# Asking for the second-layer expert weights on ScalarE's queue in a hybrid decoder block

## The reference, cut to what matters

```python
def clamped_swiglu(u):
    glu, lin = jnp.split(u, 2, axis=-1)
    glu = jnp.minimum(glu, SWIGLU_LIMIT)
    lin = jnp.clip(lin, -SWIGLU_LIMIT, SWIGLU_LIMIT)
    return glu * jax.nn.sigmoid(SWIGLU_ALPHA * glu) * (lin + 1.0)

def expert_block(args):
    xblk, e = args
    u = xblk @ w1[e] + b1[e]                 # w1[e]: 1024 x 2048, 8.39 MB
    return clamped_swiglu(u) @ w2[e] + b2[e] # w2[e]: 1024 x 1024, 4.19 MB
...
return jnp.einsum('tkd,tk->td', yb[slot].reshape(t, TOP_K, d), gates)
```

## Time and profile before

| | us |
|---|---|
| median of 3 runs | 1315.1 (1312.94 to 1317.31) |
| the profiled execution, its own time | 1317.5 |
| its span | 1315.7 |
| experts' part, start of the first expert's first layer to the end of the span | 387.4 to 1315.7 |
| DMA rate in the experts' part | 429 to 430 GB/s |

### The profile page before, as it was taken

One profiled execution on the slowest core, in us unless ns is written; L12 is line 12 of the kernel. 1 busy time (PEld: TensorE's weight loads), 2 busy tenths in 40 slices (PEclk: granted clock), 3 DMA queues, 4 the chain that ended last, 5 costly groups with the idle time before them and its releaser, 6 DMA issues.

```text
span 1315.7 us, 23661 instructions
## 1 busy us (share of the span) xinstructions
PE 1226.7 (93%) x10440; PEld 637.8 (48%) x10441; DVE 308.0 (23%) x615; ACT 214.9 (16%) x346; POOL 55.9 (4%) x33
## 2 busy tenths in 40 slices
PE   8999999999999999998989989898988989898897
PEld 6777888888653433333433333343333333343332
DVE  2464433233151211111111111121111111121112
ACT  4531221311040110010100000010100001110001
POOL 0800120000020000000000000000000000000000
PEclk9999999999989999999999999999999999999999
DMA  9521232246779999999999999999999999999994
GB/s 301 192 69 61 89 109 67 67 130 225 319 291 391 422 434 424 430 429 430 435 426 434 422 432 427 430 430 431 428 429 432 428 431 429 432 430 428 433 426 205
DMA packets 55077, 450.03 MB, mean 342 GB/s; under 512 B 5808, under 2 KB 23728, under 8 KB 35472
## 3 DMA queue, kind: packets, MB, share of 16 engines
q1 hardware_dynamic: 51936, 446.85, 82.0%
q10 hardware_dynamic: 3088, 2.37, 0.7%
HBM read 448.16 MB, written 1.05 MB: 341 GB/s over the span
## 4 chain that ended last, share of the span: by engine, by line
PE 64%; DMA 31%; DVE 3%; issue 1%; ACT 0%; SPq 0%; DVEq 0%
DMA ring<-in_exp_w 31%; PE ps L1061 21%; PE sums L557 17%; PE ps L1096 10%; PE sums L1036 3%; PE ps L1026 2%; PE sums L643 2%; PE ps L643 2%; PE sums L941 1%; PE ps L941 1%; PE ps L645 1%; PE ps L1074 1%; DVE work L2034 1%; PE ps L1083 1%; PE ps L1003 1%
## 5 line engine op out<-in xcount | busy, mean ns | idle before, releaser
L1061 PE MATMUL ps<-ring,work 128*64 128x512 f32 x2048 | 468.5, 615 | 49.3 <-DMA ring<-in_exp_w 48.5
L1061 PEld LDWEIGHTS ps<-ring,work 128*64 128x64 f32 x2048 | 155.0, 141 | 346.8 <-issue 295.9
L557 PE MATMUL sums<-work,ring 128*128 128x256 f32 (+1 forms) x1120 | 243.3, 384 | 0.6 <-DVE work L1564 0.6
L1096 PE MATMUL ps<-ring,work 128*64 128x512 f32 x1024 | 225.1, 592 | 0.0
L557 PEld LDWEIGHTS sums<-work,ring 128*128 128x128 f32 (+1 forms) x1120 | 199.7, 186 | 33.1 <-issue 3.5
L1422 ACT ACTIVATE work<-work 128x512 f32<-128x512 f32 x32 | 20.1, 629 | 733.7 <-DVE work L2023 733.7
L2023 DVE TENSOR_SCALAR work<-ps 128x512 f32<-128x512 f32 x32 | 22.1, 692 | 496.7 <-PE ps L1061 496.7
L1096 PEld LDWEIGHTS ps<-ring,work 128*64 128x64 f32 x1024 | 72.5, 136 | 129.6 <-issue 129.6
L2039 DVE COPY work<-ps 128x512 f32<-128x512 f32 x32 | 22.1, 692 | 208.2 <-PE ps L1096 208.2
L1026 PEld LDWEIGHTS ps<-sel,work 128*128 128x128 bf16 x1536 | 53.7, 118 | 24.3 <-issue 24.3
L1036 PE MATMUL sums<-work 64*128 64x512 f32 x256 | 63.6, 615 | 0.0
(11 more groups left out here) (275 smaller groups left out, 792.6 us busy)
## 6 DMA issues: line engine op xcount, KB each, us to landing
ring<-in_exp_w SPq DMA_DIRECT2D x112, 2048.0 KB, 30.4
ring<-in_exp_w SPq DMA_DIRECT2D x40, 4096.0 KB, 29.3
ring<-in_w_in SPq DMA_DIRECT2D x8, 2048.0 KB, 9.5
ring<-in_w_in SPq DMA_DIRECT2D x16, 1024.0 KB, 7.4
ring<-in_w_out SPq DMA_DIRECT2D x2, 2048.0 KB, 9.9
ring<-in_w_in SPq DMA_DIRECT2D x1, 1152.0 KB, 7.7
work<-in_x SPq DMA_DIRECT2D x2, 512.0 KB, 4.6
work<-in_x ACTq DMA_DIRECT2D x2, 512.0 KB, 4.0
```

The lines of the kernel that those rows point to most:

```text
L557: last = mm(bank_of(b)[width * g:width * g + width, 0:T], chunk(n)[:, k, c0:c0 + width], XN[:, k, :], start=k == 0, stop=k == KT - 1)
L1061: last = mm(ps[4 + part][64 * half:64 * half + 64, :], xe[:, k * CAP:(k + 1) * CAP], ring[:, slot(u, k), part * D + half * 512:part * D + ...
L1096: last = mm(ps[7][64 * half:64 * half + 64, :], lhs, ring[:, slot(u, 8 + j), i * D + half * 512:i * D + half * 512 + 512], start=False, st ...
```

## The change

The function `load_w2` moves out of SyncE's stream and takes the engine that asks as its first argument. SyncE keeps every first-layer block, and the second-layer block of expert 0. The second-layer blocks of the experts 1 to 31 are asked for by ScalarE: in the turn of expert e, right behind the sigmoid and ahead of the copies of `xe` and `actT`, two halves of C of expert e+1, with the same waits on `w_used` as before (22 and 24 counted from the expert's turn, which is 10 and 12 of the expert after). Since places and semaphores depend on the expert's number modulo 4, ScalarE's loop over the 32 experts is written out in fours, and the last four stand behind the loop, where the last expert asks for nothing.

```diff
+        def load_w2(eng, e, u, j):
+
+            g = group(u, 2)
+            src = exp_w2[0, bass.ds(e, 1), j * 4 * P:(j + 1) * 4 * P, :].rearrange(
+                "a (p s) n -> p (a s n)", s=4)
+            dst = ring[:, GROUP[g] + 2 * j:GROUP[g] + 2 * j + 2, :].rearrange("p s n -> p (s n)")
+            eng.dma_start(dst, src).then_inc((group_in, w2_half_in)[j][g], 16)
...
-            def load_expert(e, it, u, first_j=0):
+            def load_expert(e, it, u, first_j=0, second=False):
...
-                for j in range(2):
-
-                    sp.wait_ge(w_used, it * 12 + 2 * j + 10)
-                    load_w2(e, u, j)
+                if u == 0 and second:
+                    for j in range(2):
+
+                        sp.wait_ge(w_used, it * 12 + 2 * j + 10)
+                        load_w2(sp, e, u, j)
...
-                    with sp.Fori(0, E // 4) as i:
+                    for u in range(4):
+                        load_expert(u, r * E + u, u, 0, u == 0)
+                    with sp.Fori(1, E // 4) as i:
...
-                with act.Fori(0, E) as e:
-                    it = r * E + e
+                def take_expert(it, e, u, following=True):
+
                     act.wait_ge(glu_ready, it + 1)
                     af(sig, glu, ACT.Sigmoid, scale=ALPHA).then_inc(sig_ready, 1)
+                    if following:
+                        for j in range(2):
+                            act.wait_ge(w_used, it * 12 + 2 * j + 22)
+                            load_w2(act, e + 1, (u + 1) % 4, j)
                     act.wait_ge(gathered, it + 2)
                     af(xe, ps[6][:, :], ACT.Copy).then_inc(xe_ready, 1)
                     act.wait_ge(act_turned, it + 1)
                     af(actT, ps[4][:, :], ACT.Copy).then_inc(at_ready, 1)
+
+                with act.Fori(0, E // 4 - 1) as i:
+                    for u in range(4):
+                        take_expert(r * E + i * 4 + u, i * 4 + u, u)
+                for u in range(4):
+                    take_expert(r * E + (E - 4 + u), E - 4 + u, u, u < 3)
```

More of the change, by code:

```diff
@@ L479, in _ @@
             load_w1(0, 0, 1)
-            load_w2(0, 0, 1)
+            load_w2(sp, 0, 0, 1)
             sp.wait_ge(blk_done, len(blocks))
@@ L483, in _ @@
             sp.wait_ge(w_used, 16)
-            load_w2(0, 0, 0)
+            load_w2(sp, 0, 0, 0)
             load_w1(1, 1, 0, 1)
```

## The result

The changed kernel took 1327.15 us (median of 6 runs, 1322.85 to 1330.21) where the kernel before took 1316.12 (6 runs on the same chips): a ratio of 1.0078 with a 95% interval of 1.0065 to 1.0092, so 8.6 to 12.1 us slower. The forecast was 9 us slower, 1324 from a median of 1315.1. The profiled execution took 1328.85 us, its span is 1327.0, 11.3 us over that of before. Six executions of the changed kernel spread over 7 us, so of a single trace a us or two can be chance.

A forecast was written before the change was run, and what follows sets the result against it. The experts' part was taken as bound by DMA bytes at 430 GB/s. Terms 0 (ScalarE), 0 (later asks), 0 (SyncE) and +9.0 (byte order) on the median of 1315.1 gave 1324 us, range 1309 to 1333.

The forecast's parts named there:

- ScalarE's time: Two asks per expert, 0.75 us, fit in ScalarE's 2.3 us of idle time between sigmoid and copy: 0 us.
- Rival 4: ScalarE is held by its asks, so copies and second layer come late: up to 22 us, 1337 us; chance 0.03.
- Asks later: Second-layer asks go out 4.8 and 1.8 us later for expert 31, but the DMA engines do not run dry: 0 us.
- SyncE's side: SyncE loses two asks and two waits per expert, but no first-layer block is asked for sooner: 0 us.
- The order of the bytes: On its own queue, second-layer block C overtakes first-layer block B, so PE's first layer of expert 31 ends later: +9.0 us.
- Rival 1: Both DMA queues are served as one common line in order of asking, so nothing moves: 1315 us; chance 0.13.
- hand sum: Block arrivals worked: C of expert 31 through first, last half of B seen by PE at 1298.6: +9.0 us.
- D: The end of the weight transfers, put at 1296.2 us and expected to stay there.
- the way from D to the last landing: Time from the end of transfers until PE sees the last block: 2.4 us, 1296.2 to 1298.6.
- the two steps behind that landing: Two first-layer steps of expert 31 left on PE after B's last half: 3.5 us, ending at 1302.1.
- rival 3: DMA rate falls 1% from queue switching, 1333 us, or PE's lowered clock costs up to 3 us, 1327; chance 0.09.
- Rival 2: Two queues raise the DMA rate; 1% is worth 8.8 us: 1306 with order kept, 1315 with order turned; chance 0.15.

The follow-up runs named there:

- the pair of experiments: Changed kernel with only experts 1 to 28's second-layer blocks on ScalarE's queue: 1317.22 us, ratio 1.0002 to the kernel before; with only 29 to 31's: 1326.57 us, 1.0076.
- the experiment with three experts: Changed kernel with second-layer blocks of experts 1 to 28 on SyncE's queue, only 29 to 31 on ScalarE's: 1326.57 us, ratio 1.0076 to the kernel before.

## Why the prediction was right

*ScalarE's time, 0.* Right: sigmoid to copy unchanged at 2.90 us. The two asks take 0.82 us together (0.75 forecast). Rival 4 is out.

*Asks later, 0.* Right, and shown by itself: asks 5.4 and 2.6 us later on one queue give 1.0003.

*SyncE's side, 0.* Nothing in the traces speaks of a gain there. It was not tested alone.

*The order of the bytes, +9.0.* Right in mechanism and place. C at a half or a third of the rate: 116 packets to 116, 73 to 66. The waits begin at 505 us (near 500 forecast), sit on B, and the last one ends at 1299.1 (1298.6 forecast), two steps ahead of the end of the first layer. The loss is a lead that is lost once: moved back for the last three experts it is gone, made for the last three alone it is whole. Rival 1, one common line, is out by the packet counts and by the pair of experiments. One step of the hand sum came out otherwise, at no cost: C was not through first, but landed beside B (1299.3 and 1299.1).

*The size.* By the medians it is 11.0 us for 9.0. By the traces two terms were too small. The traces are to be compared from the start of the experts' part, since the part ahead of it, which the change does not touch, was 1.35 us shorter in the changed kernel's trace (387.4 before):

```profile
386.03 2.83 PE L1064 MATMUL ps<-ring,work 128*64 128x512 f32 x6 [0.83 <-ACT work L1414]
```

So the experts' part took 1315.7 - 387.4 = 928.3 us before and 1327.0 - 386.0 = 941.0 after, 12.7 us more, where the forecast had 9.0. The bytes ran out when they were forecast to. The windows from 1290 us on (they stand at the end of this document) give 1290 + (5 x 390 + 115 + 49 + 16 + 16)/430 = 1295.0, which is 909.0 us after that start; D was 1296.2, or 908.8. The first term that was too small is the way from D to the last landing. It was put at 2.4 us, and PE started again only at 1299.18, 4.2 us after. Why the tail is longer is open; in the experiment with three experts the same way was 2.2 us (1290 + (5 x 423 + 410 + 148 + 66)/430 = 1296.4, to 1298.62).

The second is the two steps behind that landing. They were put at 3.5 us and took 5.3 (1299.18 to 1304.46), since after the wait of 3.79 us the granted clock was 0.50, that is 1.2 GHz:

```profile
1300.00:1301.00 1.00, 1.00 (x6) 0.36 (x4) 0.00 (x0) 0.00 (x0) 0.00 (x0) 0.50 0.00 0
```

I had this cost as part of rival 3, at up to 3 us, and left it out of the likeliest sum; with a period's wait of 2.9 us and the row of 16.94 in place of 13.90 at hand it belonged in. The two terms, 4.2 for 2.4 and 5.3 for 3.5, give 3.6 of the 3.7 us that the sum lacks. In the experiment with three experts the last wait was only 1.21 us, the clock stayed up, and its experts' part took 1324.8 - 387.7 = 937.0 us, 8.7 over before, close to the forecast's 9.0. But both terms are read from one execution each. The medians put that kernel and the changed one level (1.0076 and 1.0078), and of the changed kernel 11.0 us over before, so how often the tail and the clock cost this much is not shown.

*The rate.* It stayed at 430 GB/s with two full queues, in 420 to 1290 us of both kernels. Rival 2 is out for these packets, and so is the part of rival 3 that let the rate fall. The Trainium skill's rule (DMA: Bandwidth & Descriptors, Rules for kernel authors) that spreading over queues brings no bandwidth agrees with the 430 here. Its rule of turns by packet (section Queues, rings and completion order) agrees with 116 to 116. By the sum, the turns themselves cost 9 of the 11 us here, at an unchanged rate.

No version run here beats the kernel before. Its blocks come in the order in which PE wants them, and the end is set within 1 us by B of expert 31: with PE waiting for B's halves to the end, the experts' part was 0.3 us shorter (928.0 to 928.3).

## What to carry to other kernels

Where transfers are the bound, as at 430 GB/s here, a second queue is no second road: it is a change of the order in which bytes arrive, and what is wanted last may come first. Look for two full queues whose transfers are wanted at different times, and read the shares from the packet counts of each queue. A loss of this kind is paid once and not per turn, so test it by switching the last few turns alone; shorter times to landing are no sign of a gain.

## What the runs showed of the hardware

Two queues that are both full are served in turn by packet, not by bytes: 271 and 272 packets carried 8.29 and 1.97 MB. A queue's share can so be set by the size of its contiguous runs.

The rate went a little with that size: 430 GB/s with 16 and 32 KB packets, 428 with 16 KB throughout, on one queue as on two, 427 with 8 KB packets for a third of the bytes (0.7% less, 6 us here). The rows of the one queue with 16 KB throughout and of the 8 KB packets:

```profile
420.00:1290.00 870.00, 794.43 (x4952) 299.36 (x4949) 142.50 (x300) 92.02 (x120) 0.00 (x0) 1.00 1.01 428
420.00:1290.00 870.00, 794.14 (x4878) 304.23 (x4876) 141.59 (x298) 61.15 (x96) 0.00 (x0) 0.96 1.01 427
```

The 16 engines do not end together. In the changed kernel the rate fell to a trickle over the last microseconds, and PE's last wait ended at 1299.1:

```profile
1290.00:1295.00 5.00, 5.00 (x26) 1.52 (x22) 0.00 (x0) 0.00 (x0) 0.00 (x0) 1.00 0.92 390
1295.00:1296.00 1.00, 0.39 (x2) 0.00 (x0) 0.00 (x0) 0.00 (x0) 0.00 (x0) 1.00 0.27 115
1296.00:1297.00 1.00, 0.00 (x0) 0.00 (x0) 0.00 (x0) 0.00 (x0) 0.00 (x0) 1.00 0.12 49
1297.00:1298.00 1.00, 0.00 (x0) 0.00 (x0) 0.00 (x0) 0.00 (x0) 0.00 (x0) 1.00 0.04 16
1298.00:1299.00 1.00, 0.00 (x0) 0.00 (x0) 0.00 (x0) 0.00 (x0) 0.00 (x0) 1.00 0.04 16
```

All but 0.2 MB were in by 1295, and still PE waited for its block until 1299.1. This is the tail that the forecast had too short; which engines lag, and why, is open.
